# First two weight units of each stage split into places of their own, and the program's last half in pairs of columns

## The reference, cut to what matters

```
for i in range(2):
    h = rms_norm_2(x, norm_mix_pre[i])
    h = sliding_window_attention(h, ...) if i == 0 else chunked_sgu(h, ...)
    x = x + rms_norm_2(h, norm_mix_post[i])
    h = conv_gated_ffn(rms_norm_2(x, norm_ffn_pre[i]), ...)
    x = x + rms_norm_2(h, norm_ffn_post[i])
return x
```

## Time and profile before

| | us |
|---|---|
| median of 3 runs | 2382.92 |
| lowest, highest | 2382.34, 2559.71 |
| the profiled execution: its own time | 2379.86 |
| the profiled execution: span | 2378.1 |
| PE busy in the span (11622 matmul records) | 2279.4 (96%) |
| POOL busy, DVE busy, ACT busy | 1051.1, 1163.3, 1009.0 |
| mean granted TensorE clock | 0.988 |

### The profile page before, as it was taken

One profiled execution on the slowest core, in us unless ns is written; L12 is line 12 of the kernel. 1 busy time (PEld: TensorE's weight loads), 2 busy tenths in 40 slices (PEclk: granted clock), 3 DMA queues, 4 the chain that ended last, 5 costly groups with the idle time before them and its releaser, 6 DMA issues. The chain is left out here.

```text
span 2378.1 us, 29013 instructions
## 1 busy us (share of the span) xinstructions
PE 2279.4 (96%) x11622; PEld 1895.8 (80%) x11622; DVE 1163.3 (49%) x1765; ACT 1009.0 (42%) x1878; POOL 1051.1 (44%) x800
## 2 busy tenths in 40 slices
PE   7989988999999999999999999989999999999997
PEld 4768766777888888888888888868888888788887
DVE  3676877845532122457575334351343346724254
ACT  4675566545442233455453222363332235422223
POOL 1444333443454444632445444444344443554543
PEclk9989999999999999999999999999999999999999
DMA  7221232356222222311123222222222222222221
GB/s 281 80 71 72 107 120 93 133 179 237 74 104 91 104 100 95 104 65 54 46 79 107 100 95 95 101 89 89 89 89 89 90 88 72 106 90 96 98 103 57
DMA packets 42792, 239.80 MB, mean 101 GB/s; under 512 B 5153, under 2 KB 7201, under 8 KB 17313
## 3 DMA queue, kind: packets, MB, share of 16 engines
q1 hardware_dynamic: 39456, 231.23, 27.1%
q10 hardware_dynamic: 3200, 6.71, 1.0%
HBM read 226.38 MB, written 8.39 MB: 99 GB/s over the span
## 5 line engine op out<-in xcount | busy, mean ns | idle before, releaser
L2468 POOL TENSOR_TENSOR WL<-RAW,WH 128x512 fp32r<-128x512 f32 (+1 forms) x724 | 957.5, 1350 | 1202.6 <-ACT WH L1253 1191.0
L706 PE MATMUL PS<-HHI,WH 128*128 128x512 f32 (+1 forms) x1688 | 658.0, 390 | 13.3 <-DVE HLO L1801 8.7
L706 PE MATMUL PS<-HHI,WL 128*128 128x512 f32 (+1 forms) x1688 | 639.9, 379 | 0.0
L706 PE MATMUL PS<-HLO,WH 128*128 128x512 f32 (+1 forms) x1688 | 639.9, 379 | 0.0
L1253 ACT ACTIVATE WH<-RAW 128x512 fp32r<-128x512 f32 (+1 forms) x724 | 398.9, 612 | 411.3 <-PE PS L706 389.3
L706 PEld LDWEIGHTS PS<-HHI,WH 128*128 128x128 f32 x1688 | 319.8, 189 | 92.1 <-issue 14.5
L706 PEld LDWEIGHTS PS<-HHI,WL 128*128 128x128 f32 x1688 | 319.4, 189 | 60.4
L706 PEld LDWEIGHTS PS<-HLO,WH 128*128 128x128 f32 x1688 | 320.1, 190 | 56.9 <-issue 1.9
L706 PE MATMUL PS<-UF,WH 128*128 128x512 f32 (+1 forms) x832 | 224.0, 357 | 0.0
L1795 DVE TENSOR_TENSOR T<-PS,R 128x512 f32<-128x512 f32 x112 | 76.9, 689 | 215.0 <-PE PS L706 204.4
L706 PEld LDWEIGHTS PS<-UF,WH 128*128 128x128 f32 x832 | 148.3, 189 | 22.8
(11 more groups left out here) (324 smaller groups left out, 3223.1 us busy)
## 6 DMA issues: line engine op xcount, KB each, us to landing
RAW<-in_wts SPq DMA_DIRECT2D x190, 1024.0 KB, 4.8
FW<-in_wts SPq DMA_DIRECT2D x6, 1024.0 KB, 17.4
spill<-T SPq DMA_DIRECT2D x24, 256.0 KB, 3.2
RAW<-in_wts SPq DMA_DIRECT2D x8, 768.0 KB, 4.1
GT<-spill SPq DMA_DIRECT2D x20, 256.0 KB, 4.8
X<-in_xt SPq DMA_DIRECT2D x2, 1024.0 KB, 9.1
out_x<-X SPq DMA_DIRECT2D x16, 128.0 KB, 1.7
X<-in_xt SPq DMA_DIRECT2D x2, 768.0 KB, 9.5
```

The costliest lines, as they stand in the source:

```text
L706: return e.matmul(o_, l, r, start=start, stop=stop)
L2468: return e.tensor_tensor(o_, a, b, f)
```

## The change

1. **Places for eight units.** The first two units of `mlp` (w1 0, 1), `f0` (fi 0, 1), `sgu` (sv 0, 1) and `f1` (fi 22, 23) leave the two turning slots and get places `WHH`, `WLH` of 16 KB in memory whose last reader is long past or is the unit before the tail (`spare`). The slots turn over the other units. Three places in ACT's list that waited for the old stage's last unit before they wrote `UP` or `UF` now wait for b.
2. **Order at the four inner boundaries.** ACT splits two quarters of a behind `squares(0, 0)`, two behind `squares(0, 1)`, and all of b behind `squares(0, 2)`, ahead of `table()` and `squares(0, 3)`. POOL splits a around `add(0, 1)` and `add(0, 2)`, then b, then does `add(1, 1)`, `add(1, 2)`. Nothing is split between the `high`s.
3. **Squares of X.** Their sum is kept in PSUM bank 6 (only the last goes to `T0[3]`), and the unit after b is split by ACT between the squares 1 to 4.
4. **Before `sgu`.** The sum of half 1 stands behind k = 3 and not k = 5, the whole sum behind the first four columns of the next pair of units, and the banks of `sv` turn over seven and not six.
5. **The end.** ACT multiplies `Y` by its gain (`gained`). DVE and POOL work on pairs of columns with the root broadcast: POOL pairs 0 and 1 of half 0 and pair 0 of half 1, DVE the rest. The last two columns are taken and squared singly, `SS` is folded to 256 wide ahead of them, and PE sums in three parts. The output leaves in 8 writes of 256 KB.

```
+        self.slots()
         self.steps = placed((self.projections(), (0, 1)), (self.gate_c(), GATE_C), (self.decays(0), DECAY[0]), (self.decays(1), DECAY[1]),
                             (self.recurrences(), RECUR), (self.attention(), ATTEND))
 
-    def slot(self, i):
-        return self.rank[i] % 2
-
-    def before_in_slot(self, i):
-        n = self.rank[i]
-        return self.dense[n - 2] if n >= 2 else None
+    def slots(self):
+
+        at = self.at
+        self.heads = [at["w1", 0], at["w1", 1], at["fi", 0], at["fi", 1], at["sv", 0], at["sv", 1], at["fi", 22], at["fi", 23]]
+        turns = [i for i in self.dense if i not in self.heads]
+        self.slot = {i: n % 2 for n, i in enumerate(turns)}
+        self.before_in_slot = {i: turns[n - 2] if n > 1 else None for n, i in enumerate(turns)}
...
-        self.take(six, *[(at["sv", 2 * j + 1], tb) for j in range(6) for tb in range(4)])
+        self.take(six + [7], *[(at["sv", 2 * j + 1], tb) for j in range(6) for tb in range(4)])
...
 
+    spare = [(16, ("w", U["out", 1])), (0, ("w", U["up", 3])), (32, ("w", U["wo", 1])), (0, ("logits2", 15)),
+             (16, ("w", P.unit["f0", "dn", 0, 3])), (48, ("w", P.unit["f0", "dn", 1, 3])), (20, ("mix", 23)), (48, ("w", P.unit["sgu", "dn", 4, 1]))]
+    WH = {i: WH2[s] for i, s in P.slot.items()}
+    WL = {i: WL2[s] for i, s in P.slot.items()}
+    for i, (at_, _) in zip(P.heads, spare):
+        WH[i] = place(f"WHH{i}", q0 + at_ * KB, [2048], F32R)
+        WL[i] = place(f"WLH{i}", q0 + at_ * KB + 8 * KB, [2048], F32R)
+
+    def w_free(i):
+
+        if i in P.heads:
+            return spare[P.heads.index(i)][1]
+        return None if P.before_in_slot[i] is None else ("w", P.before_in_slot[i])
+
+
...
-            for k in range(8):
-                q.wait_ge(*at(("x_post", "f1", k, hf)))
-                e.dma_start(half(xout[:, k, :], hf), half(X[:, k, :], hf)).then_inc(*up("out", ("out", k, hf), by=16))
-        q.wait_ge(*at(("out", 7, 1)))
+            for p in ((2, 0, 3, 1), (1, 2, 0, 3))[hf]:
+                q.wait_ge(*at(("x_post", "f1", p, hf)))
+                e.dma_start(pair_of(xout, p, hf), pair_of(X, p, hf)).then_inc(*up("out", ("out", p, hf), by=16))
+        q.wait_ge(*at(("out", 3, 1)))
 
...
                         t.then_inc(*up("psum", ("tail", name, k // 2, hf), *([("w", i)] if hf and k % 4 == 3 else [])))
+                    elif (name, k, hf) == ("f1", 6, 1):
+                        t.then_inc(*up("psum", ("tail_six",)))
                     holds(b, ("y_tail", name, k // 2, hf))
...
+                if (hf, k) == (0, 3):
                     sums_half("f0", 1)
         holds(SUMS, ("x_post", "f0", 7, 1))
-        sum_whole("sgu", 6, T0[3][:, :], ("ss2", "sgu", 7))
         for p in range(1, 6):
             for r in range(0, 8, 4):
                 for tb in range(4):
                     for k in range(r, r + 4):
                         wide(p, tb, k, "h", "sgu", k, 1)
+                    if (p, r, tb) == (1, 0, 0):
+                        sum_whole("sgu", 6, T0[3][:, :], ("ss2", "sgu", 7))
...
         ffn("sgu", "f1")
-        sums_half("f1", 1)
+        free(ROOT[1])
+        q.wait_ge(*at(("folded",)))
+        mm(PS[:, ROOT[1], 0:256], ones, SS[:, 0:256], True, False)
+        for k in (6, 7):
+            q.wait_ge(*at(("sq_last", k)))
+            t = mm(PS[:, ROOT[1], 0:256], ones, half(T0[0], k - 6), False, k == 7)
...
 
+            def roots(hf):
+
+                r, s = PS[:, ROOT[hf], 0:256], half(T0[3], hf)
+                q.wait_ge(*at(("sum", n, hf)))
+                e.activation(s, r, ACT.Ln, scale=1.0 / 1024, bias=EPSC[:, 0:1]).then_inc(*up("a_norm", ("ln", n, hf)))
+                q.wait_ge(*at(("ln", n, hf)))
+                e.activation(r, s, ACT.Exp, scale=-0.5).then_inc(*up("a_norm", ("root", n, hf)))
+                q.wait_ge(*at(("root", n, hf)))
+                e.activation(s, s, ACT.Exp, scale=-0.5).then_inc(*up("a_norm", ("root_copy", hf)))
+
+            def gained(hf, k):
+
+                y = half(Y[:, k, :], hf)
+                q.wait_ge(*at(("sq_last", k) if hf and k > 5 else ("sqp", n, hf, k // 2)))
+                e.activation(y, y, ACT.Copy, scale=post[n](k)).then_inc(*up("a_norm", ("gained", hf, k)))
+
...
                 split(t1, p)
+            if nx is None:
+                for p in range(4):
+                    if p == 3:
+                        table()
+                    squares(0, p)
+                    gained(0, 2 * p)
+                    gained(0, 2 * p + 1)
+                roots(0)
+                table()
+                squares(1, 0)
+                gained(1, 0)
+                gained(1, 1)
+                for p in (1, 2):
+                    q.wait_ge(*at(("y_tail", n, p, 1)))
+                    if p == 2:
+                        q.wait_ge(*at(("ssa", n, 1, 1)))
+                    e.activation(PS[:, 6, :].rearrange("p (k t) -> p k t", k=2), pair_of(Y, p, 1), ACT.Square).then_inc(
+                        *up("a_norm", ("sqp", n, 1, p)))
+                    gained(1, 2 * p)
+                    gained(1, 2 * p + 1)
+                for k in (6, 7):
+                    q.wait_ge(*at(("y_last", k)))
+                    e.activation(half(T0[0], k - 6), half(Y[:, k, :], 1), ACT.Square).then_inc(*up("a_norm", ("sq_last", k)))
+                    gained(1, k)
+                roots(1)
+                return
+            squares(0, 0)
+            split(a, 0)
+            split(a, 1)
+            squares(0, 1)
+            split(a, 2)
+            split(a, 3)
+            squares(0, 2)
             for p in range(4):
-                if p == 3:
-                    table()
-                squares(0, p)
+                split(b, p)
+            table()
+            squares(0, 3)
             root(0)
             table()
             squares(1, 0)
+            high(0, 0)
             squares(1, 1)
-            if nx is None:
-                squares(1, 2)
-                squares(1, 3)
-                root(1)
-                return
-            split(a, 0)
-            high(0, 0)
-            split(a, 1)
-            high(0, 1)
-            split(a, 2)
-            high(0, 2)
-            split(a, 3)
-            squares(1, 2)
-            high(0, 3)
-            high(0, 4)
-            split(b, 0)
-            squares(1, 3)
-            high(0, 5)
-            split(b, 1)
-            high(0, 6)
-            split(b, 2)
-            high(0, 7)
+            for k in range(1, 8):
+                high(0, k)
+                if 4 + k < 5:
+                    split(b, 4 + k - 1)
+                if k in (2, 4):
+                    squares(1, 2 if k == 2 else 3)
             root(1)
-            split(b, 3)
             for k in range(8):
                 high(1, k)
             if nx != "mlp":
@@ -1354,11 +1411,14 @@
                         q.wait_ge(*at(("ss2", nx, k - 2)))
...
                     elif k < 2:
                         q.wait_ge(*at(("ssa", n, 1, 3)))
-                    e.activation(T0[1 + k % 2 if k else 3][:, :], X[:, k, :], ACT.Square).then_inc(*up("a_norm", ("sq2", nx, k)))
+                    dst = T0[1 + k % 2][:, :] if k else PS[:, 6, :]
+                    e.activation(dst, X[:, k, :], ACT.Square).then_inc(*up("a_norm", ("sq2", nx, k)))
+                    if 1 <= k < 5:
+                        split(P.after(b), k - 1)
+            else:
+                split_after(b)
             if nx != "mlp":
...
+                q.wait_ge(*at(P.hidden("mlp")(p) if p > 1 else ("w", U["w1", 1])))
                 e.activation(UP[p % 2][:, n, 0, :], TQ[2 + n % 2][:, :], ACT.Copy).then_inc(*up("h_hi", ("up_hi", p, n)))
...
 
-        ffn("f0", 0, ("w", U["wo", 3]))
...
 
+            def product(hf, p, b, emptied):
+
+                q.wait_ge(*at(("root", n, hf)))
+                q.wait_ge(*at(emptied))
+                q.wait_ge(*at(("gained", hf, 2 * p + 1)))
+                r = PS[:, ROOT[hf], 0:256].unsqueeze(1).to_broadcast([128, 2, 256])
+                tt(PS[:, b, :].rearrange("p (k t) -> p k t", k=2), pair_of(Y, p, hf), r, MUL).then_inc(*up("d_norm", ("post", n, p, hf)))
+
+            def pair_residual(hf, p, b):
+                q.wait_ge(*at(("post", n, p, hf)))
+                x = pair_of(X, p, hf)
+                tt(x, PS[:, b, :].rearrange("p (k t) -> p k t", k=2), x, ADD).then_inc(*up("d_norm", ("x_post", n, p, hf)))
+
+            def add_square(p):
+                q.wait_ge(*at(("sqp", n, 1, p)))
+                q.wait_ge(*at(("ssa", n, 1, 1) if p > 1 else ("sqp", n, 1, 0)))
+                tt(SS[:, :], SS[:, :], PS[:, 6, :], ADD).then_inc(*up("d_norm", ("ssa", n, 1, p)))
+
+            def take_last(k):
+                q.wait_ge(*at(("tail", n, 3, 1) if k == 7 else ("tail_six",)))
+                y = half(Y[:, k, :], 1)
+                tt(y, half(PS[:, BANK["tail", n, k, 1], :], 1), y, ADD).then_inc(*up("d_ev", ("y_last", k)))
+
```

(78 more changed lines are left out.)

25 lines of the change are left out of this document (12 added, 13 removed).

## The result

The changed kernel takes 2380.03 us by the median (2372.9 to 2385.54), the kernel before 2383.64 beside it (2379.43 to 2386.18 but for one run of 2559.71, which is left out of the ratio), 20 runs each. The ratio is 0.9983, 95% interval 0.9975 to 0.9992: 4 us less, between 2 and 6. That is far within 2%, and above the predicted range of 2359 to 2378. The profiled execution of after has an own time of 2383.91.

What follows compares the result with a forecast made beforehand. PE, busy 96% of the span, was taken as the bound, so only its idle time and the end could be won. 23.5 - 10.9 - 1.7 + 3.0 = 13.9 us less gave 2366.0 or 2369.0, named 2368, range 2359 to 2378.

Steps and rivals of the forecast that it cites:

- The heads: The four unit heads behind the boundaries: moving POOL's splits away lets VectorE recover and ends PE's waits, 23.5 us gained.
- the first head: Head from `out` to `mlp`: 2.6 us of gaps go, 1.7 of clock comes back, 0.3 refill, 4.6 in all.
- the third: Head from `f0` to `sgu`: 7.6 us of waits go with b's last quarter early; 11.5 gained in all.
- The tail's wait: In every tail PE waits 2.3 to 3.4 us for the late sum of half 0, 10.9 together, with `add(0, 3)` at 1.41.
- if the sum's waits are absent or over 4 us: Sign of a wrong forecast, at PE's sums in the tails, where waits of 2 to 3.5 us each were expected.
- The clock: Stretches at 1.2 GHz behind the new PE gaps in the tails: one of four counted, 1.7 us, bounds none and 6.8.
- The end: Behind PE's last tile: earlier root and fewer VectorE instructions, less 0.7 for the last write, give 3.0 us, bounds 2.2 and 3.9.
- The sum: Whole program: heads, tail wait, clock and end, 23.5 - 10.9 - 1.7 + 3.0 = 13.9 us gained.
- 1: Rival: the tail's wait for the sum doesn't come, so the gain is 23.5 + 3.0, time 2356; chance 0.12.
- 2: Rival: heads don't recover, VectorE's pace being the cause, 2383; same if places come free late, a not split ahead; chance 0.13.
- 3: Rival: b's load holds ACT and the squares behind it in each tail; 2389 at twice the landing time; chance 0.05.
- a quarter held back: If POOL were the one blocked, each stretched b quarter is 0.2 us longer, 4 in all, reaching into the heads: 2372.

Runs made afterwards that it cites:

- e5: Kernel before with only the change of the program's end (part 5), nothing of parts 1 to 4: 2379.31 us, ratio 0.9982 to before.
- e6: e3 with part 4 taken back (six banks, sums of half 1 and whole sum placed as before): 2362.01 us, ratio 0.9906 to before.
- e1: Changed kernel with the last square of half 0 put in PSUM bank 6 at the inner boundaries: 2364.09 us, ratio 0.9923 to before.
- e8: Kernel before with only the places of part 1, every list keeping its order: 2384.55 us, ratio 0.9997 to before.
- e4: Kernel before with only a delay: ScalarE repeats the last square of half 0 eight times at inner boundaries: 2412.62 us, ratio 1.0125 to before.
- e2: Changed kernel with b's four splits moved behind table load and last square in ScalarE's list: 2366.51 us, ratio 0.9927 to before.
- e3: Changed kernel with both the last square in PSUM and b's splits behind it: 2357.12 us, ratio 0.9892 to before.
- e10: Changed kernel with GpSimd's splits of b waiting for VectorE's add of the last square of half 0: 2365.64 us, ratio 0.9917 to before.

## Why the prediction was wrong

The mechanisms were the ones named; two terms of the sum were mis-sized, and they hang together: the add in the tail, 5.5 us too little, and the slow clock behind the gaps, 8.9 us too little.

- **The heads: right in size, in part by luck.** 25.0 measured, 23.5 forecast; by head 5.1, 4.1, 11.7, 4.1 against 4.6, 3.7, 11.5, 3.7. `low_half` is back at its quiet duration, PE's waits for POOL's `WL` in the head of `sgu` fell from 5.4 to none, with 0.5 new behind its end. Two reasons given were not right or not whole. In the first head 1.7 of the 4.6 were to come from the clock, and e5 shows that head as long without the slow stretch: all of it was VectorE's pace. And of the third, the text says that the 7.6 us go "because b's last quarter no longer stands behind the root". e6 has b early and every `low_half` there at 0.48, and PE waits 2.0 us for one of them all the same and 2.9 for the sum of X's squares, until part 4 moves the sums in PE's list. VectorE's timeline of after in the head of `f1`, and two lines of PE's waits over the program:

```profile
2000.78 0.48 DVE L1861 SCALAR_TENSOR_TENSOR HLO<-X,V,HHI 128x256 fp32r<-128x256 f32 x1
```

```profile
PE PS L723 <- DVE SS L1855: 17.8, 5, 4.5
...
PE PS L723 <- DVE HLO L1861: 1.6, 2, 0.8
```

  The 17.8 are the four gaps of 16.4 and one of 1.5 in the end.
- **The tail's wait: the step that failed.** The text says "so I take 1.41 and not 0.69" for `add(0, 3)`. 1.41 was the row of an add beside one split. Here it starts beside a row of four that follow one another without a pause, and it took 3.98, 1.01, 2.57 and 3.86. A duration read beside a neighbour belongs to that neighbour's length; the prediction had written down the row of four itself ("and then b's for 5 us"). The rest of the chain (landing, splits, table, square) held: landings 4.7, 5.2, 6.1 and 4.8 us after issue, and with the add at 0.69 (e1) the gaps are 7.4 for the 8.0 worked out. With the long add they were 16.4 for 10.9. The bound was missed on one side: "if the sum's waits are absent or over 4 us" stood among the signs of being wrong, but no price for it in the range.
- **The clock: mis-sized, the largest error.** One stretch of four was counted, 1.7 us, because one of four heads with gaps had one. That count is itself one trace's: the same heads had two in e5 and three in e8. And their gaps were many and mostly short, 1.61 at most in that of the earlier trace rows; these are single ones of 2.8 to 4.5 us, and all four had a stretch, three of them 6.8 us and not 3.4: 10.6. The upper bound, 6.8, was too low also, since it took a stretch to be 3.4 long. e4 shows the price with nothing else changed. In e1 the gaps of 1.3 us had none and those of 2.4 one of 3.4 us each.
- **The end: 2.15 for 3.0**, at the lower bound of 2.2. VectorE's part came as worked out (3.0 less from root to last instruction). The root came 0.25 earlier and not 0.7, and the last write costs 1.05 more and not 0.7: the 256 KB writes land in 2.2 us where those of 128 KB took 1.7. GpSimd's pair cost nothing that the rows show.
- **The sum.** 25.0 - 16.4 - 10.6 + 2.15 is nothing by the rows (1 us slower with the 1.2 behind the third head), 3.6 gained by the medians, 13.9 forecast.
- **The rivals.** 1 fell: the wait came in every tail. 2 fell in its mechanism, though its time, 2383, is nearly what was measured, which is chance: the heads did recover. Its second half, that the places matter, is answered by e8. 3 fell for the load, but its shape, a chain ahead of the sum made longer with the whole tail behind it, is what happened, in VectorE and not in the DMA.

The Trainium skill's page "SBUF — State Buffer" (Who interferes with whom) says that the port pair shared by the two engines is an exclusive lock and that the order of issue decides who blocks. The trace agrees on the kind: VectorE's add loses against GpSimd (0.69 to 5.33), and in e2's other three tails GpSimd's first split was the one held back, by 0.35 to 0.55 us, where the prediction put 0.2 on a quarter held back. But the prediction let the lock last one instruction, and here the waiting add was passed over between GpSimd's instructions two times in `out` and `sgu`, once in `f0` and three times in e2's `attn`.

Left open: why the add of `attn` in after got through after 1.01 when the others waited for the row's end. It started 0.46 us before the end of the split under way, the others 0.8 to 1.1 before; with one case against four that is an observation and no cause. Open too is how often it goes one way or the other from run to run. It could explain why after's runs spread over 12.6 us, those of before over 6.8, but only the profiled execution shows the adds.

## What to carry to other kernels

Before you move a row of GpSimd instructions, look at what VectorE does in the new stretch: an instruction with both operands in SBUF may wait there for the whole row, so if PE waits for it, put one operand in PSUM, or make GpSimd wait for it. Price a new gap of PE with the slow clock behind it: here a gap of 4.7 us cost 7, while gaps of 1.3 us cost 1.4 to 1.5 (e1 against e3). And when a change has a good and a bad half, run the halves: the same idea with its cause mended gave 1.3% where the change as written gave what its end alone gives.

## What was not expected of the hardware

- A VectorE add of 512 with two SBUF operands, 0.69 us alone, was started inside a row of GpSimd splits of 1.25 us each in five cases. In four it took 2.57 to 5.33 and ended some 0.55 us after the row's last; in the fifth it took 1.01, and the row went on.
- With single gaps of PE of 4.5 to 5.3 us in the tails (eight) there was always a stretch of 6.8 us at clock 0.50, which began inside the gap; with gaps of 2.4 to 2.8 us one of 3.4 us in four cases (after, e1 twice, e10) and none in a fifth (e10, 2.37); with gaps of 0.6 to 1.6 us in the tails, none.
- The same code ahead of the first boundary took 614.1 to 622.1 us from one profiled execution to the next, most of it by how long it ran at the lower clock. Differences of whole traces below some 5 us say little in this kernel. Boundaries with the same waits agree to 0.2 us, unless a slow stretch falls in one: e8's `sgu` was 2.6 longer by that alone.
